# Two of three mLSTM chunk products on split rounded operands, with the heads' order rewritten

## The chip, the cores and the metric

The kernel runs on one core of a Trainium2 chip. The metric is the device time of one execution in microseconds (us), the median of several runs.

## What is computed

A trunk of two layers on x (1024 positions, width 1024). Layer 0 is an mLSTM mixer, layer 1 a pooling mixer; the change touches the chunk recurrence of layer 0 alone. Cut to that:

```python
proj = x @ w_in                                   # xm, z, o, gates
xc = silu(causal_dwconv(xm, conv_w, conv_b))
q = einsum(xch, w_q) * DK**-0.5;  k = einsum(xch, w_k);  v = einsum(xmh, w_v)
# 8 heads, DK 128, DV 256, 8 chunks of 128 positions; carry (C, n, m)
def step(carry, inp):
    ...
    s = einsum("bhtd,bhsd->bhts", qq, kk) * w_intra
    num = (einsum("bhts,bhsv->bhtv", s, vv)
           + w_inter[..., None] * einsum("bhtd,bhdv->bhtv", qq, C))
    den = s.sum(-1) + w_inter * einsum("bhtd,bhd->bht", qq, n)
    h = num / maximum(abs(den), exp(-m_t))[..., None]
    ...
    C_new = w_c[..., None, None] * C + einsum("bhs,bhsd,bhsv->bhdv", w_s, kk, vv)
```

## The kernel before

Everything large is a fp32 product made of rounded operands: each operand is split into a high part (rounded, type fp32r) and a low part (the rest, fp32r too), and `split()` in the TensorE block (L2774, L2775, L2776) issues three matmuls, high by high, high by low, low by high. The high part of a tile is written by ScalarE (`in_high`, L1153, and its like), the low part by VectorE as raw minus high (`in_low`, L1870).

Layer 0 walks through its input projection in 24 pairs of blocks, three pairs for a head (X_OF, Z_OF, O_OF), each pair in seven products (a Strassen scheme), 12 matmuls of 128x512 for a product. `PRODUCTS_A` is their order, `AT_A` its inverse; operands lie in a ring of four (`inb`). Between the products stands the rest of a head h:

- After product (O_OF, 5): `values(h)` makes v in 48 matmuls of 128x256, then `query_or_key` makes q and k in 24 of 128x512. Their operands are the parts of the head's qkv weights (`qkv`, high and low), of xm (`xm_hi`, and its low part in `xx_lo`) and of xc (`xc_hi`, and its low part in the other head's `xx_lo`).
- `CHUNK_AFTER` and `chunk_after` then put one chunk behind each of the next eight products. `chunk(h, c)` is `outputs(h, c)` and `scores(h, c + 1)`. `outputs` has three products in full fp32, 128x257 (v has 256 columns and one of ones): sT by v into `ps_intra` (L2946), qw by `state` added to it (L2949, not for chunk 0), and kw by v into `ps_state` (L2952, not for chunk 7). `scores` transposes a piece of k (L2931) and makes k by q for the next chunk (L2934), fp32 as well.
- Around it: `weighted_s` (VectorE, L1963) multiplies the scores by the decay weights `wgt` (ScalarE, `decay`, L1276) into sT; `weighted_k` (ScalarE, L1280) makes kw; `take_num` (ScalarE, L1284) copies the output; `next_state` (VectorE, L1991, L1993) updates `state`; `chunk_stats` (L1999), `scales` (L1969 to L1977), a power on GpSimd (`power`, L1031) and `norm_scale` (L1983, L1984) make the normalisation; the y_ and h_ steps make the branch output.

There is one sT, one kw, one wgt and one state, so each step waits for the reader of the one before. Every engine runs its instructions strictly in the order written down by hand: `first_half(h)`, `second_half(h)` and `next_head(h)` for ScalarE and for VectorE, where first_half(h) holds the chunks 1 to 7 of head h - 1; `first_layer_out` does the last head; long lists ahead of the loop do the start. SyncE issues the loads in one queue in the same way (`load_qkv`, `load_in`, `load_rows`, `store_h`). What reaches an engine early waits there behind whatever stands first.

## Time and profile before

| | before |
|---|---|
| median of 3 runs | 1404.59 us (1404.48 to 1404.92) |
| profiled execution, its own time | 1404.74 us |
| profiled execution, span of the trace | 1403.0 us |
| granted TensorE clock, mean | 0.998 of full speed |
| TensorE matmul busy | 1388.0 us, 99% |
| VectorE busy | 1119.1 us, 80% |
| ScalarE busy | 727.1 us, 52% |
| GpSimd busy | 152.4 us, 11% |

The span is what the trace covers of the one profiled execution, 1.7 us less than that execution's time. Layer 0 with its eight heads fills about the first 700 us of it; the recurrence stands between 89 and 699 us. A matmul's record is longer than its slot, since matmuls overlap: its cost is read from start to start. A fp32 matmul leaves two records.

### The profile page before, as it was taken

The numbers are of one execution on the slowest core, as the hardware profiler recorded it, in microseconds if no ns is written. First come the engines' busy times: TensorE is split into PE (matmuls) and PEld (weight loads), VectorE is DVE, ScalarE is ACT, GpSimd is POOL, SyncE is SP. The second block draws the span as 40 slices with busy tenths as digits, with TensorE's granted clock in tenths as the row PEclk, the third lists the DMA queues.
The fourth block names the chain that finished last, engine by engine and source line by source line (L and its number), as shares of the span: only waits on it lengthen the run. The fifth ranks groups of instructions, "written<-read, shape, count | busy, mean of one in ns | idle before, by whom it ended". The sixth has DMA issues, their size and how long they took to land.

```text
span 1403.0 us, 18567 instructions
## 1 busy us (share of the span) xinstructions
PE 1388.0 (99%) x6488; PEld 1155.2 (82%) x6488; DVE 1119.1 (80%) x1739; ACT 727.1 (52%) x1202; POOL 152.4 (11%) x251
## 2 busy tenths in 40 slices
PE   9999999999999999999999999999999999999997
PEld 7788888888888888888878888878888888888886
DVE  7988879798887978878674455797888888889976
ACT  6865646556564655656543345664333343336341
POOL 2002011110100111010000001001111111100021
PEclk9999999999999999999999999999999999999999
DMA  5024425353342534336487666444665555689661
GB/s 229 33 69 124 110 69 150 91 140 93 106 128 54 165 82 137 105 99 195 136 292 254 211 207 217 131 128 105 166 162 153 140 161 153 170 271 358 217 198 75
DMA packets 103435, 213.26 MB, mean 152 GB/s; under 512 B 10912, under 2 KB 27552, under 8 KB 102192
## 3 DMA queue, kind: packets, MB, share of 16 engines
q1 hardware_dynamic: 90544, 178.53, 38.4%
q0 software_dynamic: 12800, 33.56, 12.2%
q8 instruction: 52, 0.85, 0.2%
q14 instruction: 39, 0.32, 0.1%
HBM read 170.04 MB, written 75.56 MB: 175 GB/s over the span
## 4 chain that ended last, share of the span: by engine, by line
PE 62%; DVE 2%; DMA 1%; issue 0%; POOL 0%; ACT 0%; SPq 0%; DVEq 0%; POOLq 0%; ACTq 0%
PE wide L2774 13%; PE wide L2775 12%; PE wide L2776 12%; PE ps_state L2774 2%; PE ps_state L2775 2%; PE ps_state L2776 2%; PE ps_inter L2774 2%; PE ps_inter L2775 2%; PE ps_inter L2776 2%; PE ps_s L2774 1%; PE ps_intra L2774 1%; PE ps_s L2775 1%; PE ps_intra L2775 1%; PE ps_s L2776 1%; PE ps_intra L2776 1%; PE ps_intra L2946 1%
## 5 line engine op out<-in xcount | busy, mean ns | idle before, releaser
L2775 PE MATMUL wide<-xa,inb 128*128 128x512 f32 x576 | 224.5, 390 | 0.0
L2774 PE MATMUL wide<-xb,inb 128*128 128x512 f32 x472 | 189.3, 401 | 0.1
L2776 PE MATMUL wide<-xb,inb 128*128 128x512 f32 x472 | 184.3, 391 | 0.0
L2775 PEld LDWEIGHTS wide<-xa,inb 128*128 128x128 f32 x576 | 108.4, 188 | 19.7
L2775 PE MATMUL wide<-xa,blk 128*128 128x512 f32 x320 | 124.5, 389 | 0.0
L2776 PEld LDWEIGHTS wide<-xb,inb 128*128 128x128 f32 x472 | 88.6, 188 | 18.9
L2774 PEld LDWEIGHTS wide<-xb,inb 128*128 128x128 f32 x472 | 88.8, 188 | 18.0 <-DVE inb L1870 1.2
L2774 PE MATMUL wide<-xb,blk 128*128 128x512 f32 x256 | 99.7, 389 | 0.8 <-ACT zz L1741 0.8
L2776 PE MATMUL wide<-xb,blk 128*128 128x512 f32 x256 | 99.6, 389 | 0.0
L1789 ACT ACTIVATE wy<-wy_raw 128x1024 fp32r<-128x1024 f32 x56 | 59.4, 1062 | 61.9 <-DMA wy_raw<-y_block 61.6
L2774 PE MATMUL wide<-xa,inb 128*128 128x512 f32 x208 | 83.1, 400 | 2.8 <-DVE inb L1870 1.8
L2776 PE MATMUL wide<-xa,inb 128*128 128x512 f32 x208 | 81.2, 390 | 0.0
L2424 DVE TENSOR_TENSOR mw<-mw_raw,mw 128x1024 fp32r<-128x1024 f32 x53 | 63.0, 1220 | 20.0 <-ACT mw L1634 20.0
L2775 PEld LDWEIGHTS wide<-xa,blk 128*128 128x128 f32 x320 | 60.1, 188 | 12.5
L2677 DVE TENSOR_TENSOR wy<-wy_raw,wy 128x1024 fp32r<-128x1024 f32 x56 | 66.0, 1219 | 3.4 <-ACT wy L1789 3.1
L1646 ACT ACTIVATE blk<-a_raw 128x512 fp32r<-128x512 f32 x64 | 40.0, 627 | 44.3 <-PE wide L2776 21.6
L1923 DVE SCALAR_TENSOR_TENSOR xx<-xx,cols 128x1024 f32<-128x1024 f32 x48 | 61.4, 1280 | 1.5 <-ACT xx L1216 0.9
L1284 ACT ACTIVATE num<-ps_intra 128x257 f32<-128x257 f32 x64 | 24.6, 384 | 65.4 <-PE ps_state L2952 61.1
L1634 ACT ACTIVATE mw<-mw_raw 128x1024 fp32r<-128x1024 f32 x53 | 53.6, 1051 | 9.0 <-DMA mw_raw<-h_block 9.0
L2774 PEld LDWEIGHTS wide<-xb,blk 128*128 128x128 f32 x256 | 48.1, 188 | 11.2 <-issue 1.2
L2776 PEld LDWEIGHTS wide<-xb,blk 128*128 128x128 f32 x256 | 48.1, 188 | 9.9
L1629 ACT ACTIVATE stage<-wide 128x512 f32<-128x512 f32 x24 | 14.3, 597 | 79.1 <-PE wide L2776 78.5
(431 smaller groups left out, 3802.6 us busy)
## 6 DMA issues: line engine op xcount, KB each, us to landing
in_raw<-in_w_in SPq DMA_DIRECT2D x45, 512.0 KB, 4.3
wy_raw<-y_block SPq DMA_DIRECT2D x56, 256.0 KB, 4.4
mw_raw<-h_block SPq DMA_DIRECT2D x53, 256.0 KB, 3.4
m_sum<-in_w_out POOLq DMA_DIRECT2D x48, 256.0 KB, 4.6
h_block<-f_buf SPq DMA_DIRECT2D x48, 256.0 KB, 3.2
w_sum<-in_pool_w_out POOLq DMA_DIRECT2D x48, 256.0 KB, 4.3
a_raw<-in_pool_w_z SPq DMA_DIRECT2D x16, 512.0 KB, 4.0
a_raw<-folded SPq DMA_DIRECT2D x16, 512.0 KB, 4.4
```

Of the source, the lines that this page charges most:

```text
L1284: act.activation(num[:, c, :], ps_intra[:, 0:DV + 1], ACT.Copy).then_inc(num_taken, 1)
L1629: act.activation(dst[:, s % STAGES, :], spare_banks[spare_bank(("F", s))], ACT.Copy).then_inc(fold_taken, 1)
L1634: act.activation(hi, raw, ACT.Copy).then_inc(mw_hi, 1)
L1646: act.activation(blk_hi_at(i), block_raw(i), ACT.Copy).then_inc(blk_hi, 1)
L1789: act.activation(hi, raw, ACT.Copy).then_inc(wy_hi, 1)
L1923: ins = dve.scalar_tensor_tensor(out=xc_at(h, j), in0=xm_at(h, j, i), scalar=cols[:, at:at + 1], in1=xc_at(h, j), op0=ALU.mult, op1=ALU.add)
L2424: dve.tensor_tensor(lo, raw, hi.bitcast(F32), ALU.subtract).then_inc(mw_lo, 1)
L2677: dve.tensor_tensor(lo, raw, hi.bitcast(F32), ALU.subtract).then_inc(wy_lo, 1)
L2774: pe.matmul(dst, a[0], b[0], start=first, stop=False, skip_group_check=more)
L2775: pe.matmul(dst, a[0], b[1], start=False, stop=False, skip_group_check=more)
L2776: return pe.matmul(dst, a[1], b[0], start=False, stop=last, skip_group_check=more)
L2946: mm = pe.matmul(ps_intra[:, 0:DV + 1], sT[:, :], v, start=True, stop=c == 0)
```

## The change

`outputs` makes two of its three products on split rounded operands, each as three matmuls, hi by hi, hi by lo, lo by hi. The product with `state` stays fp32, as do the scores and the transpose.

```diff
-                mm = pe.matmul(ps_intra[:, 0:DV + 1], sT[:, :], v, start=True, stop=c == 0)
+                pe.matmul(ps_intra[:, 0:DV + 2], sT_hi[:, :], hi, start=True, stop=False)
+                pe.matmul(ps_intra[:, 0:DV], sT_hi[:, :], lo, start=False, stop=False)
+                mm = pe.matmul(ps_intra[:, 0:DV + 2], sT_lo[:, :], hi, start=False, stop=c == 0)
                 if c:
                     pe.wait_ge(state_ready, (NC - 1) * h + c)
                     mm = pe.matmul(ps_intra[:, 0:DV + 1], qw[:, tile(c)], state[:, :], start=False, stop=True)
                 if c < NC - 1:
-                    pe.wait_ge(kw_made, (NC - 1) * h + c + 1)
-                    mm = pe.matmul(ps_state[:, 0:DV + 1], kw[:, :], v, start=True, stop=True)
+                    pe.wait_ge(k_low, (NC - 1) * h + c + 1)
+                    pe.matmul(ps_state[:, 0:DV + 2], kw_hi[:, :], hi, start=True, stop=False)
+                    pe.matmul(ps_state[:, 0:DV], kw_hi[:, :], lo, start=False, stop=False)
+                    mm = pe.matmul(ps_state[:, 0:DV + 2], kw_lo[:, :], hi, start=False, stop=True)
```

The parts come from new steps. On ScalarE `weighted_k` writes kw and kw_hi, `round_s` writes sT_hi, and `round_v` rounds the upper half of v. On VectorE `low_s`, `low_k` and `low_v` write the low parts:

```diff
             def weighted_k(h, c):
                 act.wait_ge(s_full, NC * h + c + 1)
-                act.activation(kw[:, :], ps_inter[:, 0:P], ACT.Identity, scale=gcol_at(c, 3, h)).then_inc(kw_made, 1)
+                act.activation(kw[:, :], ps_inter[:, 0:P], ACT.Identity, scale=gcol_at(c, 3, h))
+                act.activation(kw_hi[:, :], ps_inter[:, 0:P], ACT.Identity, scale=gcol_at(c, 3, h)).then_inc(kw_made, 1)
+
+            def round_s(h, c):
+                act.wait_ge(s_taken, NC * h + c + 1)
+                act.activation(sT_hi[:, :], sT[:, :], ACT.Copy).then_inc(s_high, 1)
...
+            def low_s(h, c):
+                dve.wait_ge(s_high, NC * h + c + 1)
+                dve.tensor_tensor(sT_lo[:, :], sT[:, :], sT_hi[:, :].bitcast(F32), ALU.subtract).then_inc(chunk_low, 1)
+
+            def low_k(h, c):
+                dve.wait_ge(kw_made, (NC - 1) * h + c + 1)
+                dve.tensor_tensor(kw_lo[:, :], kw[:, :], kw_hi[:, :].bitcast(F32), ALU.subtract).then_inc(k_low, 1)
```

v's high parts lie in `xx_lo`; its low parts lie in `qkv`, in the place of the head's weights: for chunks 0 to 3 where the v weights were, taken straight from PSUM (`low_v(h, 0)` and `(h, 1)`, 128x512 each, ahead of the k products), for chunks 4 to 7 where the q and k weights were (`round_v(h, 0)` after k, `low_v(h, 2)`, 128x1024, then `round_v(h, 1)`). So the next head's weights are loaded later, and stand behind two `load_in` in SyncE's queue:

```diff
             def load_qkv(h):
                 if h:
-                    sp.wait_ge(k_full, 2 * h)
+                    sp.wait_ge(num_full, h * NC)
                 sp.dma_start(qkv_raw[:, 1, :], p_qkv[h, :, :]).then_inc(qkv_in, 16)
...
             for h in range(1, HEADS):
-                load_qkv(h)
                 load_in(3 * h + 1, 0)
                 load_in(3 * h + 1, 1)
+                load_qkv(h)
```

The lists of ScalarE and VectorE are written anew for the start, for each head and for the last head. Semaphores of layer 1 are shared with new ones of layer 0 by offsets; this moves no instruction.

TensorE in chunk 1 of the first head, before:

```order
L2946 MATMUL ps_intra<-xx,sT 128x257
L2949 MATMUL ps_intra<-state,qw 128x257
L2952 MATMUL ps_state<-xx,kw 128x257
L2931 MATMUL ps_inter<-ident,kT 128x128
L2934 MATMUL ps_s<-qT,kT 128x128
```

And now, in the next chunk of the same kind (the lines are those of the changed kernel):

```order
L3073 MATMUL ps_intra<-xx_lo,sT_hi 128x258
L3074 MATMUL ps_intra<-qkv,sT_hi 128x256
L3075 MATMUL ps_intra<-xx_lo,sT_lo 128x258
L3078 MATMUL ps_intra<-state,qw 128x257
L3081 MATMUL ps_state<-xx_lo,kw_hi 128x258
L3082 MATMUL ps_state<-qkv,kw_hi 128x256
L3083 MATMUL ps_state<-xx_lo,kw_lo 128x258
L3055 MATMUL ps_inter<-ident,kT 128x128
L3058 MATMUL ps_s<-qT,kT 128x128
```

Two fp32 matmuls have become six rounded ones; one fp32 matmul stands between them.

VectorE in the fourth head, from the weighting of chunk 5's scores (first row) to that of chunk 6's (second row with sT<-ps_s), before; in_low is the rows inb<-in_raw, norm_scale the two rows with small:

```order
L1963 TENSOR_TENSOR sT<-ps_s,wgt 128x128
L1870 TENSOR_TENSOR inb<-in_raw,inb 128x512
L1999 BN_STATS stats<-num 128x6
L1870 TENSOR_TENSOR inb<-in_raw,inb 128x512
L1983 TENSOR_TENSOR small<-small,rstd 128x4
L1984 SCALAR_TENSOR_TENSOR small<-mv,small 128x4
L2007 SCALAR_TENSOR_TENSOR o_buf<-o_buf,z_buf 128x512
L2013 TENSOR_TENSOR f_buf<-f_buf,z_buf 128x512
L1963 TENSOR_TENSOR sT<-ps_s,wgt 128x128
```

And now, from the last rows of `scales` (L2056 to L2058) to the low part of chunk 6's sT, on which TensorE waits:

```order
L2056 TENSOR_TENSOR small<-small 128x4
L2057 TENSOR_TENSOR small<-small,mv 128x4
L2058 TENSOR_SCALAR small<-small 128x4
L2080 BN_STATS stats<-num 128x6
L2064 TENSOR_TENSOR small<-small,rstd 128x4
L2065 SCALAR_TENSOR_TENSOR small<-mv,small 128x4
L2094 TENSOR_TENSOR f_buf<-f_buf,z_buf 128x512
L2024 TENSOR_TENSOR sT<-ps_s,wgt 128x128
L2088 SCALAR_TENSOR_TENSOR o_buf<-o_buf,z_buf 128x512
L2094 TENSOR_TENSOR f_buf<-f_buf,z_buf 128x512
L2044 TENSOR_TENSOR kw_lo<-kw,kw_hi 128x128
L2040 TENSOR_TENSOR sT_lo<-sT,sT_hi 128x128
```

`scales` has moved behind the weighting of chunk 5's scores, so norm_scale now follows it with one instruction between, and two steps of 128x512 stand between the weighting and the low part.

## Rows read from the trace of the kernel before

**Rows 1.** The page: the span, and each engine's busy time and instructions.

```profile
span 1403.0 us, 18567 instructions
PE 1388.0 (99%) x6488; PEld 1155.2 (82%) x6488; DVE 1119.1 (80%) x1739; ACT 727.1 (52%) x1202; POOL 152.4 (11%) x251
```

**Rows 2.** Busy time by stretch, fourth head: chunks, saturated stretch, all; clock, DMA.

```profile
336.73:367.25 30.52, 30.52 (x150) 25.72 (x148) 23.47 (x57) 15.94 (x38) 2.92 (x4) 1.00 0.24 61
...
376.15:410.57 34.42, 34.42 (x180) 29.41 (x179) 33.96 (x43) 22.88 (x34) 4.74 (x6) 1.00 0.55 151
...
336.73:419.31 82.58, 82.58 (x408) 69.68 (x407) 69.61 (x127) 48.54 (x90) 9.99 (x14) 1.00 0.39 109
```

**Rows 3.** Timeline of PE, first head, chunk 1 and product: start, length, instruction.

```profile
92.40 0.40 PE L2776 MATMUL wide<-xb,inb 128*128 128x512 f32 x1
92.63 0.60 PE L2946 MATMUL ps_intra<-xx,sT 128*128 128x257 f32 x2
93.07 0.59 PE L2949 MATMUL ps_intra<-state,qw 128*128 128x257 f32 x2
...
93.93 0.27 PE L2931 MATMUL ps_inter<-ident,kT 128*128 128x128 f32 x1
...
94.50 0.39 PE L2775 MATMUL wide<-xa,inb 128*128 128x512 f32 x1
...
97.00 0.60 PE L2946 MATMUL ps_intra<-xx,sT 128*128 128x257 f32 x2
```

**Rows 4.** Groups by line and shape, PE: records (two for each) and mean length.

```profile
L2946 PE MATMUL ps_intra<-xx,sT 128*128 128x257 f32 x128 | 38.3, 380 | 0.0
```

**Rows 5.** Timeline of PE: first matmul of values, and first after its 48.

```profile
74.33 0.28 PE L2774 MATMUL ps_state<-qkv,xm_hi 128*128 128x256 f32 x1
...
80.04 0.39 PE L2774 MATMUL wide<-xc_hi,qkv 128*128 128x512 f32 x1
```

**Rows 6.** Timeline of DVE, fourth head, chunks 4 and 5; scales, state, scores, stats.

```profile
352.94 0.15 DVE L1969 SCALAR_TENSOR_TENSOR small<-num,gcol 128x4 f32<-128x4 f32 x1
...
354.22 0.17 DVE L1977 TENSOR_SCALAR small<-small 128x4 f32<-128x4 f32 x1
355.31 0.48 DVE L1993 SCALAR_TENSOR_TENSOR state<-state,wc_bc,ps_state 128x257 f32<-128x257 f32 x1 [0.91 <-PE ps_state L2952]
355.70 0.28 DVE L1963 TENSOR_TENSOR sT<-ps_s,wgt 128x128 f32<-128x128 f32 x1
355.90 0.68 DVE L1870 TENSOR_TENSOR inb<-in_raw,inb 128x512 fp32r<-128x512 f32 x1
356.80 0.43 DVE L1999 BATCH_NORM_STATS2 stats<-num 128x6 f32<-128x256 f32 x1 [0.22 <-ACT num L1284]
357.15 0.67 DVE L1870 TENSOR_TENSOR inb<-in_raw,inb 128x512 fp32r<-128x512 f32 x1
357.74 0.15 DVE L1983 TENSOR_TENSOR small<-small,rstd 128x4 f32<-128x4 f32 x1
...
358.01 0.69 DVE L2007 SCALAR_TENSOR_TENSOR o_buf<-o_buf,z_buf 128x512 f32<-128x512 f32 x1
```

**Rows 7.** Timeline of POOL: the power between scales and norm_scale.

```profile
354.48 1.03 POOL L1031 TENSOR_TENSOR rstd<-small,nhalf 128x4 f32<-128x4 f32 x1 [8.48 <-DVE small L1977]
```

**Rows 8.** Timeline of ACT: weighted_k and the decay behind it.

```profile
360.47 0.36 ACT L1280 ACTIVATE kw<-ps_inter,gcol 128x128 f32<-128x128 f32 x1
360.72 0.40 ACT L1276 ACTIVATE wgt<-m_bc,gcol 128x128 f32<-128x128 f32 x1
```

**Rows 9.** Timeline of DVE, fourth head: low part of xm, first half.

```profile
403.04 1.22 DVE L1943 TENSOR_TENSOR xx_lo<-xx,xm_hi 128x1024 fp32r<-128x1024 f32 x1
```

**Rows 10.** Timeline of PE: values start, fourth head; a late product, fifth head.

```profile
404.93 0.28 PE L2774 MATMUL ps_state<-qkv,xm_hi 128*128 128x256 f32 x1
...
484.52 0.39 PE L2776 MATMUL wide<-xb,inb 128*128 128x512 f32 x1
485.04 0.50 PE L2774 MATMUL wide<-xb,inb 128*128 128x512 f32 x1
```

More of the change, by code:

```diff
@@ L341, in build @@
             bias = sA("bias", [P, 1])
+            sA("line_b", [P, 15])
+            sT_hi, kw_hi = (sA(name, [P, P], F32R) for name in ("sT_hi", "kw_hi"))
         with ExitStack() as own:
@@ L2097, in first_half @@
                 x = AT_A[3 * h + 2, 1] - 14
-                in_sum(3 * h, 3)
+                weighted_s(h - 1, 2)
                 in_join(3 * h - 1, 4)
                 next_state(h - 1, 1)
-                weighted_s(h - 1, 2)
+                chunk_stats(h - 1, 1)
+                in_sum(3 * h, 3)
+                low_s(h - 1, 2)
+                low_k(h - 1, 2)
+                y_factor_o(h - 1, 0)
+                y_factor_f(h - 1, 0)
                 gate_out_z(h - 1, 2)
                 gate_out_z(h - 1, 3)
-                y_factor_o(h - 1, 0)
@@ L2121, in first_half @@
-                in_low(x + 7)
                 chunk_stats(h - 1, 4)
-                in_low(x + 8)
                 norm_scale(h - 1, 0)
+                y_factor_f(h - 1, 1)
+                weighted_s(h - 1, 6)
                 y_factor_o(h - 1, 2)
                 y_factor_f(h - 1, 2)
-                weighted_s(h - 1, 6)
+                low_k(h - 1, 6)
+                low_s(h - 1, 6)
                 next_state(h - 1, 5)
-                chunk_stats(h - 1, 5)
                 y_factor_o(h - 1, 3)
-                in_sum(3 * h + 1, 0)
@@ L2222, in first_layer_out @@
                 in_low(AT_A[PAIRS_A - 1, 3])
+                group_lo(0)
+                weighted_s(last, 0)
+                low_s(last, 0)
                 weighted_q(last)
-                weighted_s(last, 0)
-                group_lo(0)
-                unit_lo(0)
+                low_k(last, 0)
+                low_v(last, 2)
+                gate_out_z(last, 2)
+                gate_out_z(last, 3)
+                chunk_stats(last, 0)
+                weighted_s(last, 1)
+                low_s(last, 1)
@@ L2227, in first_layer_out @@
+                next_state(last, 0)
+                low_k(last, 1)
+                unit_lo(0)
+                unit_lo(1)
+                in_join(PAIRS_A - 1, 4)
+                next_state(last, 1)
+                low_k(last, 2)
+                weighted_s(last, 2)
+                low_s(last, 2)
+                weighted_s(last, 3)
+                low_k(last, 3)
                 y_factor_o(last, 0)
                 y_factor_f(last, 0)
-                next_state(last, 0)
-                weighted_s(last, 1)
@@ L2242, in first_layer_out @@
+                unit_lo(3)
+                weighted_s(last, 4)
                 y_factor_o(last, 1)
+                next_state(last, 3)
+                low_s(last, 4)
+                low_k(last, 4)
                 y_factor_f(last, 1)
                 y_factor_o(last, 2)
-                next_state(last, 3)
-                weighted_s(last, 4)
-                chunk_stats(last, 1)
-                chunk_stats(last, 2)
+                next_state(last, 4)
+                weighted_s(last, 5)
@@ L2249, in first_layer_out @@
+                low_s(last, 5)
+                unit_lo(4)
+                low_k(last, 5)
                 chunk_stats(last, 3)
-                unit_lo(3)
-                weighted_s(last, 5)
                 scales(last, 0)
-                next_state(last, 4)
-                y_factor_f(last, 2)
-                unit_lo(4)
+                norm_scale(last, 0)
                 weighted_s(last, 6)
-                norm_scale(last, 0)
                 next_state(last, 5)
                 unit_lo(5)
+                low_k(last, 6)
@@ L2260, in first_layer_out @@
+                low_s(last, 6)
                 chunk_stats(last, 4)
+                y_factor_f(last, 2)
                 y_factor_o(last, 3)
@@ L2358, in _ @@
             in_low(15)
+            in_join(2, 2)
+            low_xc(0, 1)
+            low_xc(0, 0)
+            low_v(0, 0)
+            low_v(0, 1)
             in_join(2, 5)
-            gate_out_z(0, 1)
+            in_low(16)
+            weighted_s(0, 0)
+            gate_out_z(0, 0)
             weighted_q(0)
-            weighted_s(0, 0)
+            low_k(0, 0)
+            low_s(0, 0)
             in_sum(3, 0)
             in_sum(3, 1)
-            in_low(16)
             in_sum(3, 2)
@@ L2368, in _ @@
             next_state(0, 0)
+            gate_out_z(0, 1)
+            low_s(0, 1)
             chunk_stats(0, 0)
             in_low(17)
+            low_k(0, 1)
+            low_v(0, 2)
             for h in range(1, HEADS):
```

484 lines of the change are left out of this document (276 added, 208 removed).

## The prediction

> **What bounds the kernel now.** I read the page's busy shares first: TensorE is busy for 1388.0 of 1403.0 us, so the span is TensorE's own work and a cut of it is worth its full size unless something new makes TensorE wait [rows 1]. Then the busy time by stretch, for one head: over 82.58 us TensorE has no gap, while VectorE is busy for 69.61 and ScalarE for 48.54. But VectorE's idle time lies unevenly: in the 30.5 us of the chunks it is busy for 23.5, in the 34.4 us ahead of values for 34.0, which is no room at all [rows 2]. Last the timelines, from start to start, since records overlap and a short wait of TensorE doesn't show as a gap: one product in the fifth head starts 0.52 us after the matmul before it, where 0.23 is the slot, so about 0.3 us was lost there while VectorE ran late [rows 10]. VectorE's order is therefore the second thing to watch, TensorE's work the first.
>
> **Step 1, TensorE's matmuls.** What goes: from 92.63 to 93.93 us stand three fp32 products of 257 columns, 1.30 us, so 0.433 us each [rows 3]. What comes: values issues 48 rounded matmuls of 256 columns in 80.04 - 74.33 = 5.71 us, 0.119 us each [rows 5]; the 512 column ones run at (97.00 - 94.50) / 11 = 0.227 us [rows 3], so two columns more cost about 0.001 us, and the three matmuls of a split product 0.120 + 0.119 + 0.120 = 0.359 us. A product gains 0.074 us. There are 128 / 2 = 64 products with sT [rows 4], and by the code seven of eight chunks have one with kw, 56: 120 in all, 120 x 0.074 = **8.9 us** less on TensorE, all of it on the path.
>
> The bounds of the rate: 258 columns are shown by no row. Below lies the 256 column slot, 0.119 us; above, the 512 column one, 0.227 us, with which 240 matmuls of 258 columns would cost 26 us more. I take 0.120, since the row differs from it in two columns and nothing else.
>
> The Trainium skill, page "TensorE: Matmul & The Clock Gate", section "Back-to-back issue gap", gives a spacing of the column count divided by 2.4 GHz plus about 2.5 ns. By that a matmul of 256 or 258 columns would take about 0.110 us, a split product 0.330, and the gain would be 12 us. This trace doesn't agree: 0.119 for 256 columns and 0.227 for 512 [rows 3, 5].
>
> **Step 2, switches between the two kinds.** Into fp32 the slot is 92.63 - 92.40 = 0.23 us, so nothing is seen. Out of it: from 93.93 to 94.50 stand three records of 128 columns and one rounded matmul. A 257 column record takes 0.217, so a 128 column one about 0.108; 3 x 0.108 + 0.227 = 0.55, which leaves 0.02 for a switch there and back [rows 3]. Chunks 1 to 6 gain two switches each (the fp32 product with state now stands between rounded ones): 48 pairs x 0.02 = 1.0 us at most, 0 at least. I take **0.9 us** back, so 8.0 us remain.
>
> **Step 3, the new work of the other engines.** VectorE's price is 0.20 us for 128x128 (355.70 to 355.90) and 0.59 for 128x512 (357.15 to 357.74) [rows 6], so about 1.13 for 128x1024 (its 1.22 us record [rows 9] less the same 0.09 of overlap). A head adds 8 low_s, 7 low_k, two low_v of 512 and one of 1024: 15 x 0.20 + 2 x 0.59 + 1.13 = 5.3 us. ScalarE adds 7 second kw, 8 round_s at 0.25 to 0.36 [rows 8] and two of 1024 columns at about 1.0 each, some 6 us. Idle are 82.6 - 69.6 = 13 and 34 us of a head [rows 2], so both fit by amount. By place: low_s, low_k and low_v(h, 2) fall in the chunks, where VectorE has 7.0 us idle for 4.1 us of new work; low_v(h, 0) and (h, 1) fall between the end of values and the k products, while q is made (12 x 0.23 = 2.8 us), which covers them and the two copies out of PSUM ahead of them. The load of the next weights waits for the last chunk now and is used by ScalarE some 15 us later; behind it wait one load_in and the rows of decays, with time to spare. I cost all of these at nothing; without cover it would be the 5.3 us a head.
>
> **Step 4, the chain ahead of a chunk.** TensorE used to need one VectorE step after the scores; now it needs three in a row, weighted_s, round_s, low_s: 0.28 + 0.36 + 0.28 plus two handovers, about 1.05 us. The cover is one product, 12 x 0.227 = 2.73 us [rows 3], less some 0.17 us until the scores are in PSUM (a record outlasts its slot by 0.16). What stands between them on VectorE's list decides. Adding up the list for chunks 1 to 5 and 7, the low part comes 0.05 to 0.8 us ahead of TensorE; chunk 2 is the closest (the scores' weighting, a join, the state, the statistics, a sum: 0.20 + 0.60 + 0.39 + 0.35 + 0.60, then the low part). Chunk 6 comes out late. Put t = 0 where TensorE starts chunk 5; a chunk took 94.50 - 0.23 - 92.63 = 1.64 us [rows 3] and takes 1.64 - 0.15 + 0.02 = 1.51 now, so chunk 6 wants to start at 1.51 + 2.73 = 4.24. The scores of chunk 5 came at -2.55 (chunk 4 started 4.24 earlier, its block and 0.18 us of landing make 1.69). ScalarE writes kw twice and then sT_hi, 0.25 + 0.25 + 0.36, so low_s(5) runs at -1.65 to -1.45; state 0.39 and low_k 0.20 bring -0.85; scales takes 354.22 + 0.17 - 352.94 = 1.45, to 0.60 [rows 6]; the power starts 0.09 later and takes 1.03, to 1.72 [rows 7]. Only chunk_stats (0.35) lies beside it, so VectorE stands idle for some 0.8 us, and norm_scale starts at 1.8. Then 0.27 for it, 0.60 for y_factor_f, weighted_s at 2.67, two steps of 0.60 and low_k: low_s(6) starts at 4.27 and ends at 4.55. TensorE waits about **0.3 to 0.4 us**. In the kernel before, 3.3 us of other work lay between scales and norm_scale, and TensorE needed only the weighting. Seven heads have this list (the last one has its own, with fewer steps there): 7 x 0.4 = **2.8 us**. Bounds: 0 if each step is a little shorter than I count, 5 us if chunk 2 joins in with 0.3 us.
>
> **Step 5, the saturated stretch.** In the fourth head the low part of xm ended at 403.04 + 1.22 = 404.26, values began at 404.93 [rows 9, 10]. Behind the weighting of chunk 7, the new list has 0.6 + 0.2 + 0.35 + 0.6 us more to do (in_low, low_s, chunk_stats, in_sum) and 0.4 less (a state), 1.3 us net; of the 5.5 us that a head's VectorE idles outside the two stretches of rows 2, about a half lies there and most of it can be used, and in_low(x + 20) stands 1.1 us earlier against its neighbours. I find low_xm about 0.8 us ahead of TensorE, so no new wait; the waits of before in two heads, some 0.6 us, may go or stay. I count 0.3 us of gain, from 0 to 0.6.
>
> **The sum.** Profiled execution 1404.74 = span 1403.0 + 1.7. Less 8.9, plus 0.9, plus 2.8, less 0.3: 5.5 us less, 1399.2; the median of the runs lies 0.15 below the profiled one: **1399.0 us**, from 1396.3 (no new wait) to 1401.7 (5 us of waits, rounded matmuls as priced).
>
> **The rivals.**
> - *All is hidden.* The chain for chunk 6 fits after all and no wait comes. For it: VectorE idles 13 us a head [rows 2]. Against it: the power's 1.03 us [rows 7] has almost nothing beside it. 1404.6 - 8.3 = 1396.3 us.
> - *The gain is eaten.* The chain is late for most chunks by a little: 8.0 / 56 = 0.14 us for each chunk of 56 is enough to eat all, and my margins at chunks 1 and 2 are 0.2 and 0.05. For it: one sT, one wgt and a strict order, so that a late step of ScalarE holds VectorE too. 1404 us, within 1401.8 to 1407.4.
> - *Slower: the saturated stretch overflows.* Where the chunks' new 4.1 us aren't taken up in idle time, VectorE enters the stretch ahead of values late, and there is nothing to catch up with: 34.0 of 34.4 us are busy [rows 2]. It decides from about 0.8 us of lateness on; with 2.6 us late (half of a head's new work), 1.8 us x 7 heads = 12.6 us go. On top of the forecast, 1399.0 + 12.6 = 1412 us. The late product in the fifth head speaks for it [rows 10].
> - *The rate isn't what values shows*: 258 columns priced as 512, 1399.0 + 26 = 1425 us. Nothing but the missing row speaks for it.
>
> **How the numbers follow.** Forecast 0.58, all hidden 0.16, eaten 0.14, overflow 0.10, rate 0.02. The range goes from 1395.9 to 1404.5: it takes in the forecast, the hidden case and most of the eaten one. Some 0.2% (2.8 us) is what a measurement of this kernel tells from no change: faster means under 1401.8, slower over 1407.4. The first two cases give 0.74 less a little of the forecast's upper edge, 0.73; eaten and that edge 0.15; the last two 0.12.
>
> **What would show it.** Right: matmuls of 258 columns 0.120 us apart; blocks of chunks 1 to 6 of 1.51 us instead of 1.64; one late start a head, at chunk 6, of 0.3 to 0.4 us, released by VectorE's sT_lo; VectorE idle on GpSimd's rstd by some 0.8 us a head; no new wait at values. Wrong: the late starts elsewhere or none, a pitch of heads over 82.3 us, a rounded matmul of over 0.13 us, or a wait for the loads behind load_qkv.

## The result and the profile after

The change made the kernel slower: 1414.72 us (1412.36 to 1415.05) against 1404.53 us (1404.1 to 1404.92) of the kernel before in the same comparison, a ratio of 1.0069 with a 95% interval of 1.0052 to 1.0086. One of the ten executions of experiment 6 took 4477.9 us and is left out of its ratio; nothing else below was disturbed like that. The forecast was 1399.0, the range ended at 1404.5; the sign was wrong.

The page after, to be laid beside [rows 1]:

```profile
span 1412.6 us, 19112 instructions
PE 1387.5 (98%) x6608; PEld 1153.4 (82%) x6608; DVE 1159.2 (82%) x1883; ACT 771.8 (55%) x1338; POOL 152.4 (11%) x251
```

TensorE is busy for about as long as before, which says little here: a record of TensorE outlasts its slot, and hides short gaps. VectorE has 40 us more and is at 82% instead of 80. The place of the loss is read from TensorE's waits (line waited for, releaser: us in total, times, longest):

```profile
PE ps_inter L3094 <- ACT num L1328: 6.6, 7, 1.5
PE ps_intra L3073 <- DVE sT_lo L2040: 1.6, 4, 0.5
PE wide L2898 <- DVE z_buf L1968: 1.4, 4, 0.5
```

The first row is new and the largest. It is the turn of the normalised head's second half (`turn_head`'s third, behind the product that follows chunk 7), which waits for ScalarE's `norm_head(h-1, 1)`. "The taps" below are VectorE's steps of the convolution, `xx<-xx,cols` in the trace; the product behind them needs a join (`z_buf<-wide,z_buf`) that stands after them in VectorE's list. "Values" is the stretch of 48 matmuls that makes v, and a head's pitch is the time from its chunk 0 to the next head's.

**By head.** Adding up starts of TensorE that come more than 0.1 us late, over the seven heads from chunk 0 to chunk 0: the third turn 7.65 us (0.82 to 0.91, in two heads 1.64 and 1.66), chunk 0 2.24 (four heads), the product behind the taps 2.03 (four heads), chunk 6 1.98 (0.26 to 0.30 in each). In the kernel before it was 0.6 in all. The sum of the seven pitches went from 578.8 to 587.7 us, 8.9 of the span's 9.6. Of what is outside them, chunk 0 of the first head starts 0.46 us later (89.16 instead of 88.70), and the last head's turn waits 1.25 instead of 0.44. Windows of the fourth head, its chunks and from chunk 7 to values (length, then busy time of PE, PEld, DVE, ACT, POOL), first before, then after:

```profile
336.73:367.25 30.52, 30.52 (x150) 25.72 (x148) 23.47 (x57) 15.94 (x38) 2.92 (x4) 1.00 0.24 61
367.25:404.93 37.68, 37.68 (x173) 31.22 (x172) 35.30 (x57) 22.27 (x34) 6.33 (x7) 1.00 0.56 154
```

```profile
340.49:370.63 30.14, 30.00 (x162) 25.64 (x163) 25.60 (x69) 19.84 (x52) 2.93 (x4) 1.00 0.19 46
370.63:410.56 39.93, 38.05 (x174) 31.04 (x173) 36.64 (x60) 20.52 (x30) 6.20 (x7) 1.00 0.62 170
```

The chunks became shorter by 0.4 us, with a wait of 0.3 us at chunk 6 in them; experiment 5, which takes this wait away, makes it 0.8. The stretch behind chunk 7 became 2.25 longer, and VectorE, called full there, is idle for 3.3 us of it (2.4 before). It isn't short of time, it waits itself.

**What was right.** TensorE in chunk 1 of the first head (beside [rows 3]): matmuls of 258 and 256 columns start 0.12 us apart, and the state's fp32 product among them costs nothing to be seen (measured as the prediction did it, chunk 5 of the fourth head takes 358.84 - 0.23 - 357.12 = 1.49 us, against 1.64 before and 1.51 forecast):

```profile
93.03 0.28 PE L3073 MATMUL ps_intra<-xx_lo,sT_hi 128*128 128x258 f32 x1
93.15 0.28 PE L3074 MATMUL ps_intra<-qkv,sT_hi 128*128 128x256 f32 x1
93.27 0.28 PE L3075 MATMUL ps_intra<-xx_lo,sT_lo 128*128 128x258 f32 x1
93.39 0.59 PE L3078 MATMUL ps_intra<-state,qw 128*128 128x257 f32 x2
```

Chunk 6 of the fourth head, VectorE first, then TensorE, which should have started at 365.60:

```profile
363.07 0.16 DVE L2064 TENSOR_TENSOR small<-small,rstd 128x4 f32<-128x4 f32 x1 [0.83 <-POOL rstd L1054]
...
365.56 0.29 DVE L2040 TENSOR_TENSOR sT_lo<-sT,sT_hi 128x128 fp32r<-128x128 f32 x1
```

```profile
365.37 0.39 PE L2900 MATMUL wide<-xb,inb 128*128 128x512 f32 x1
365.90 0.39 PE L3073 MATMUL ps_intra<-xx_lo,sT_hi 128*128 128x258 f32 x1
366.12 0.28 PE L3074 MATMUL ps_intra<-qkv,sT_hi 128*128 128x256 f32 x1
```

0.30 us late, VectorE idle for 0.83 on GpSimd's power: step 4, to the place and the size. The first matmul after such a wait also takes 0.22 us to the next instead of 0.12. Its weight load starts at 365.89, together with it; that of the matmul at 365.37 started 0.22 us ahead of it.

**What was missed.** The same head behind chunk 7 (370.63). Before, where chunk 7 started at 367.25, VectorE's `scales` began at 372.71, and ScalarE's norm_head ran at 376.27:

```profile
372.11 0.68 DVE L1893 TENSOR_TENSOR inb_raw<-in_raw 128x512 f32<-128x512 f32 x1
372.71 0.16 DVE L1969 SCALAR_TENSOR_TENSOR small<-num,gcol 128x4 f32<-128x4 f32 x1
```

```profile
376.27 2.08 ACT L1289 ACTIVATE num<-num,small 128x256 f32<-128x256 f32 x4 [1.24 <-DVE small L1984]
```

```profile
379.47 0.60 PE L2963 MATMUL ps_inter<-ident,num 128*128 128x128 f32 x4
```

So it ended at 378.35 and TensorE came at 379.47: 1.1 us to spare. After, on VectorE, GpSimd, ScalarE and TensorE:

```profile
374.14 0.69 DVE L1954 TENSOR_TENSOR sum_t<-in_raw 128x512 f32<-128x512 f32 x1 [0.70 <-DMA in_raw<-in_w_in]
...
376.98 0.69 DVE L1931 TENSOR_TENSOR inb<-inb_raw,inb 128x512 fp32r<-128x512 f32 x1
377.58 0.74 DVE L2104 SCALAR_TENSOR_TENSOR o_buf<-ps_s,cols,o_buf 128x512 f32<-128x512 f32 x1
378.24 0.68 DVE L1968 TENSOR_TENSOR xx<-wide,xx 128x512 f32<-128x512 f32 x1
378.84 0.16 DVE L2050 SCALAR_TENSOR_TENSOR small<-num,gcol 128x4 f32<-128x4 f32 x1
```

```profile
380.39 1.40 POOL L1054 TENSOR_TENSOR rstd<-small,nhalf 128x4 f32<-128x4 f32 x1 [11.61 <-DVE small L2058]
```

```profile
382.22 2.08 ACT L1328 ACTIVATE num<-num,small 128x256 f32<-128x256 f32 x4 [1.49 <-DVE small L2065]
```

```profile
382.57 0.39 PE L2900 MATMUL wide<-xb,inb 128*128 128x512 f32 x1
384.44 0.63 PE L3094 MATMUL ps_inter<-ident,num 128*128 128x128 f32 x4 [1.48 <-ACT num L1328]
```

`scales` starts 8.21 us behind chunk 7 instead of 5.46. 0.70 of the 2.75 is a wait for a load: it is issued only 1.5 us ahead of chunk 7, since it waits for in_low(x+8), which now stands behind chunk 7's weighting, and it took 5.0 us in this head and in the seventh, 3.5 to 4.2 in the others. 1.26 are in_low(x+11) and y_turned(h-1, 1), which now stand ahead of scales; the rest comes of the other y_ steps that do, y_turned(h-1, 0) and y_finish(h-1, 0). In heads without the wait for the load norm_head starts 10.8 us behind chunk 7 instead of 9.0, and the 1.1 us to spare become 0.8 of wait.

**The waits behind the taps** have a second cause beside the longer list. Once a head GpSimd lays a mask over `m_bc`, and VectorE's steps beside it take longer. In the first, third, fourth and fifth heads the mask makes one of them longer by 0.61 to 0.83 us, and these are the four heads where the product behind the taps is late; in the second, sixth and seventh it costs 0.24 or 0.25, and the product is in time. The fifth and the sixth head have VectorE's steps in the same order and to within 0.06 us at the same distance from chunk 7 up to this place. The mask in each, then VectorE beside it:

```profile
468.19 1.10 POOL L1083 TENSOR_SCALAR_AFFINE_SELECT m_bc<-m_bc 128x1024 f32<-128x1024 f32 x1 [1.80 <-DMA qw<-wi_rows]
...
553.14 1.14 POOL L1083 TENSOR_SCALAR_AFFINE_SELECT m_bc<-m_bc 128x1024 f32<-128x1024 f32 x1 [3.58 <-DMA qw<-wi_rows]
```

```profile
468.39 1.44 DVE L1931 TENSOR_TENSOR inb<-in_raw,inb 128x512 fp32r<-128x512 f32 x1 [0.86 <-ACT inb L1176]
...
552.63 0.69 DVE L1931 TENSOR_TENSOR inb<-in_raw,inb 128x512 fp32r<-128x512 f32 x1 [0.86 <-ACT inb L1176]
553.23 0.75 DVE L2104 SCALAR_TENSOR_TENSOR o_buf<-ps_inter,cols,o_buf 128x512 f32<-128x512 f32 x1
553.90 0.92 DVE L1931 TENSOR_TENSOR inb<-in_raw,inb 128x512 fp32r<-128x512 f32 x1
```

Two steps on the fifth head is 0.55 us behind the sixth, and its product behind the taps is 0.5 us late. In the kernel before the mask cost VectorE 0.9 us in four heads and no product behind the taps was late: the shift of the list used up the spare time, and the mask's place then decided.

### The profile page after: what moved, and what is told of

The parts are those of the page before. It is cut to its first block, busy times and chain, and to the rows that moved or that the text cites. A ratio compares the mean times of both kernels' runs of the same rounds, so it can differ in the third digit from the quotient of the medians.

```text
span 1412.6 us, 19112 instructions
## 1 busy us (share of the span) xinstructions
PE 1387.5 (98%) x6608; PEld 1153.4 (82%) x6608; DVE 1159.2 (82%) x1883; ACT 771.8 (55%) x1338; POOL 152.4 (11%) x251
## 4 chain that ended last, share of the span: by engine, by line
PE 73%; issue 12%; DVE 6%; DMA 3%; ACT 2%; POOL 2%; SPq 0%; DVEq 0%; POOLq 0%; ACTq 0%
PE wide L2898 15%; PE wide L2900 15%; PE wide L2899 15%; PE ps_state L2898 3%; PE ps_state L2900 3%; PE ps_state L2899 3%; PE ps_inter L2899 2%; PE ps_inter L2898 2%; PE ps_inter L2900 2%; DMA in_raw<-in_w_in 2%; PE ps_intra L2900 2%; PE ps_s L2898 2%; PE ps_intra L2898 2%; PE ps_s L2900 2%; PE ps_s L2899 2%
## 5 line engine op out<-in xcount | busy, mean ns | idle before, releaser
L1931 DVE TENSOR_TENSOR inb<-in_raw,inb 128x512 fp32r<-128x512 f32 x70 | 49.9, 725 | 8.7 <-ACT inb L1176 8.6
```

The lines of the kernel that those rows point to most:

```text
L1931: dve.tensor_tensor(inb[:, i % RING_A, 1, :], in_source(i), inb[:, i % RING_A, 0, :].bitcast(F32), ALU.subtract).then_inc(in_lo, 1)
```

## The experiments

Times are medians; each ratio is to the kernel before, run beside it. Where waits and pitches are given, they are those of the one profiled execution. Run 3 is that of experiment 3, and so on. Lines left out inside a code cut are marked with dots. A wait "at the turn" is the third turn's.

**1. The rounding by itself.** In the kernel before, the first seven heads get the three rounded matmuls on constant tiles of the input, so that nothing has to make the parts; what these heads compute is left out by it.

```diff
-                mm = pe.matmul(ps_intra[:, 0:DV + 1], sT[:, :], v, start=True, stop=c == 0)
...
+                def three(b, last):
+                    pe.matmul(b[:, 0:DV + 2], known[0], known[1], start=True, stop=False)
+                    pe.matmul(b[:, 0:DV], known[0], known[1][:, 0:DV], start=False, stop=False)
+                    return pe.matmul(b[:, 0:DV + 2], known[0], known[1], start=False, stop=last)
+
+                if h < HEADS - 1:
+                    mm = three(ps_intra, c == 0)
...
```

> The kernel before, where in heads 1 to 7 the two products of outputs are three rounded matmuls each on constant tiles of the input (258, 256 and 258 columns), with the old lists and the old waits; nothing makes the split parts, so the branch of these heads is not computed. It measures steps 1 and 2 alone. Theory (the matmuls gain what was forecast, the loss is elsewhere): 105 of the 120 products, 7/8 of 8.0 us less, 7.0 us, about 1397.6 us, block of chunks 1 to 6 1.51 us instead of 1.64. Rival (258 columns or the switches cost more in this place): 1402 us or over.

1398.23 us, ratio 0.9956 (0.9942 to 0.9970), as expected. Steps 1 and 2 hold: the rounding is worth 6.3 us in seven heads, where they give 7.0. The loss is in the rest.

**2. The reverse.** The changed kernel with fp32 products of the high parts.

```diff
-                pe.matmul(ps_intra[:, 0:DV + 2], sT_hi[:, :], hi, start=True, stop=False)
-                pe.matmul(ps_intra[:, 0:DV], sT_hi[:, :], lo, start=False, stop=False)
-                mm = pe.matmul(ps_intra[:, 0:DV + 2], sT_lo[:, :], hi, start=False, stop=c == 0)
+                whole = hi.bitcast(F32)[:, 0:DV + 1]
+                mm = pe.matmul(ps_intra[:, 0:DV + 1], sT_hi[:, :].bitcast(F32), whole, start=True, stop=c == 0)
...
```

> The changed kernel with its lists, its splits and all its waits, but each split product done as one fp32 matmul of the high parts (257 columns); the low parts are made and not used. TensorE's work is that of the kernel before again. Theory (at the turn TensorE waits for a chain of VectorE and DMA steps that doesn't hang on its own speed in the chunks): of the 8 us that the matmuls cost more, most disappear in the waits, 1414 to 1418 us. Rival (each part adds by itself): 1414.7 + 8 = 1422.7 us.

1418.95 us, 1.0098 (1.0083 to 1.0114): one us above what the waits' theory gave, well under the 1422.7 of plain adding. From chunk 7 to values the seven heads take 273.9 us, the same as with rounded products; the chunks take 216.8 instead of 210.9. So the new orders and steps cost about 14 us over the kernel before, and the rounding gives back 4 here, since some of it runs into waits.

**3. The norm's scales earlier.** `scales(h-1, 1)` directly behind `chunk_stats(h-1, 7)`, `norm_scale(h-1, 1)` behind `in_sum(3h+1, 1)`, on ScalarE `norm_head(h-1, 1)` ahead of `in_high(x+12)`.

```diff
                 chunk_stats(h - 1, 7)
+                scales(h - 1, 1)
                 y_finish(h - 1, 0)
                 in_sum(3 * h + 1, 0)
                 in_sum(3 * h + 1, 1)
+                norm_scale(h - 1, 1)
...
-                scales(h - 1, 1)
                 y_finish(h - 1, 1)
-                norm_scale(h - 1, 1)
...
```

> The changed kernel with the second scales and norm_scale of a head moved ahead of the four in_sum (scales directly behind chunk_stats of chunk 7) and norm_head(h - 1, 1) moved ahead of in_high(x + 12) on ScalarE. Theory A (the loss is TensorE waiting 0.8 to 1.7 us a head at the third turn for norm_head, because scales, the power and norm_scale come late in VectorE's list): the 8.6 us of these waits go, nearly nothing comes back: 1404.5 to 1407 us. Theory B (VectorE is simply full, the overflow rival: lateness moves on to the products ahead of values): the waits move there, under 3 us gained, 1411.5 us or over.

1411.37 us, 1.0043 (1.0028 to 1.0058). No wait at the turn is left in the seven heads, but the product behind the taps now comes 5.3 us late in all instead of 2.0. Between the theories, and close to the second: the turn's wait was real, and nearly half of what it gave was lost some 10 us further on.

**4. The load earlier.** `in_low(x+8)`, whose operand the next load overwrites, behind `next_state(h-1, 5)`.

> The changed kernel with in_low(x + 8) moved from behind weighted_s(7) to behind next_state(5), so that SyncE's load of the next block, which waits for it, is issued some 1.5 to 2 us earlier. Theory A' (the late load holds the first in_sum, and with it scales): VectorE's wait of 0.7 us for the load goes, the third turn's wait falls by about 0.7 us a head, 7 x 0.7 = 4.9 us, 1410 us. Rival (the load only just covers other lateness, the list itself is too long there): under 1.5 us gained, 1413 us or over.

1410.37 us, 1.0042 (1.0027 to 1.0057), the time that was expected. The turn's waits fell from 7.65 to 4.51 us, less than the expected 4.9, and those behind the taps rose from 2.0 to 3.5 in this execution, in which the mask costs VectorE 0.78 to 0.88 us in six heads; in these the product is late, in the other it is not.

**5. Chunk 6's list.** `norm_scale(h-1, 0)` behind `weighted_s(h-1, 6)`, and `y_factor_f(h-1, 2)`, one of the two steps of 128x512 ahead of low_k and low_s, behind `next_state(h-1, 5)`.

```diff
                 chunk_stats(h - 1, 4)
-                norm_scale(h - 1, 0)
                 y_factor_f(h - 1, 1)
                 weighted_s(h - 1, 6)
+                norm_scale(h - 1, 0)
                 y_factor_o(h - 1, 2)
-                y_factor_f(h - 1, 2)
                 low_k(h - 1, 6)
                 low_s(h - 1, 6)
                 next_state(h - 1, 5)
+                y_factor_f(h - 1, 2)
...
```

> The changed kernel with norm_scale(0) moved behind weighted_s(6), and y_factor_f(2) behind next_state(5), so that low_s(6) comes about 1 us earlier. The wait of 0.3 us at chunk 6 goes in seven heads. Theory A says that this gives little or nothing by itself, since TensorE then comes to the third turn earlier and waits there for the same VectorE chain, which is held by the load and the list: 1413.5 to 1415 us. Rival (each wait is lost by itself and adds): 7 x 0.3 = 2.1 us, 1412.5 us.

1409.7 us, 1.0037 (1.0023 to 1.0052). The waits at chunk 6 are gone and the chunks take 208.1 us instead of 210.9. That is 2.8, and 5.0 came off the time; the turn's waits fell too (7.65 to 5.87). A gain at one place isn't eaten here; both theories had expected less.

**6. The three together.**

> The changed kernel with the three moves of a1, a2 and a3 together. After the single moves, theory H (head of line: TensorE's waits come from a few VectorE steps that stand in the list behind a DMA landing, a power or the taps, not from a lack of VectorE time): the third turn's and chunk 6's waits go together, those at chunk 0 (2.2 us in all) and at the product behind the taps (2 to 4 us) stay: 1402 to 1405 us. Theory B (VectorE is full): its lateness collects at the product behind the taps, 1407 us or over.

1405.46 us, 1.0004 (0.9995 to 1.0014): the kernel before is reached, at the upper edge of what the theory of places gave (1402 to 1405). Pitches of 82.1 to 82.9 us; what is left lies at chunk 0 (1.6 in all) and behind the taps (4.0).

**7 and 8. Two further moves, alone and on top.** `in_sum(3h+3, 0)` behind chunk 0's low parts, and `in_join(3h+1, 5)` ahead of the last tap.

```diff
-                in_sum(3 * h + 3, 0)
                 low_s(h, 0)
                 low_k(h, 0)
+                in_sum(3 * h + 3, 0)
```

> The changed kernel with the last two moves of a5 alone: in_sum(3h + 3, 0) behind low_s(0) and low_k(0), and in_join(3h + 1, 5) ahead of the third tap. Theory H: the waits at chunk 0 (2.2 us) and behind the taps (2.0 us) go, and nothing is given back at the turn beyond 1 us, since their stretches lie far apart: 1410.5 to 1412 us. Rival (one VectorE chain through the whole head): 1413.5 us or over.

> The five moves: those of a4, in_join(3h + 1, 5) ahead of the third tap, and in_sum(3h + 3, 0), which waits for a load, behind low_s(0) and low_k(0). VectorE and ScalarE do the same work as in the changed kernel. Theory H: no wait of size is left in the heads, pitch 81.6 to 82.0 us, and the time comes to what m1 measured for the matmuls alone, 1396.5 to 1400 us, faster than the kernel before. Theory B: VectorE's 5 us more a head have to show, pitch 82.5 us or over, 1404 us or over.

1416.57 us (1.0084, 1.0070 to 1.0097) alone, 1406.87 us (1.0020, 1.0011 to 1.0029) on top: 1.9 and 1.4 us more than without them, and both numbers as the rivals had them. The waits at chunk 0 went, but the join now stood in VectorE's list before what it waits for was done and held the list up (VectorE is idle ahead of it for about 1 to 1.5 us), and TensorE waited at values in every head:

```profile
PE ps_state L2898 <- DVE xx_lo L2004: 3.3, 7, 0.5
```

So the first of the two moves does what it should at its place, and the second is bad.

**9. SyncE's order.** `load_in(3h+2, 0)` ahead of `load_qkv(h)`.

```diff
-                load_qkv(h)
                 load_in(3 * h + 2, 0)
+                load_qkv(h)
```

> The changed kernel with two lines of SyncE's list exchanged in each head: load_in(3h+2, 0) is issued ahead of load_qkv(h), which waits until the last chunk's scales for the rows are read. Theory (a queue held by its head): the late load holds in_low(x+14) on VectorE, 1.58 us idle in one head of the last trace, and through it the join and the product behind the taps, where TensorE waits 0.35 to 0.63 us in four heads; these go, the third turn's waits of 0.8 us a head stay. Time 1412.5 to 1414.0 us, 0.5 to 2 us under the changed kernel. Rival (the late product comes from VectorE's own list, and the load has no part in it): no change, 1414.7 within 0.5.

1414.68 us, 1.0068 (1.0056 to 1.0081): no change, as the rival had it. The load isn't issued sooner (5.7 us behind chunk 7 in most heads, as without the exchange), since it waits for VectorE's four sums anyway. The product behind the taps is late in six heads here, and again in those six where the mask makes a VectorE step longer by 0.6 us or more; in the fourth head it costs 0.27, and the product is in time.

**10. Five moves:** 3, 4, 5, the first of 7, and 9.

> The changed kernel with five moves in the orders and no operation taken out or added: scales and norm_scale of the second half directly behind their sums and ScalarE's norm_head(1) ahead of in_high; norm_scale(h-1, 0) behind weighted_s(6); in_low(x+8) behind next_state(5); in_sum(3h+3, 0) behind low_s(h, 0) and low_k(h, 0); load_in(3h+2, 0) ahead of load_qkv(h). Theory A (single places of the order are late, VectorE's sum of work is not the bound): the three moves tried together left a pitch of 82.7 us a head, with waits at chunk 0 (0.1 to 0.5) and behind the taps (0.2 to 1.0); the two further moves take most of them, pitch 81.7 to 82.1 us, time 1398 to 1402 us, faster than the kernel before. Theory B (the stretch ahead of values is full, so what is saved at one place comes back at another): the waits only change place, time 1404 to 1407 us as with three moves.

1404.93 us (1402.60 to 1409.20), 1.0005 (0.9996 to 1.0014): taken alone, this is what the theory of a full VectorE gave (1404 to 1407), and not the 1398 to 1402 of the theory of places. Chunk 0 is in time in every head; behind the taps 4.5 us are left, in one head 0.14 and in another 1.53.

**11. Seven moves:** also `in_join(3h+1, 5)` behind the last tap and, in the last head, norm_head ahead of a load's rounding.

> The last kernel with two more moves: in_join(3h+1, 5) on VectorE directly behind the last tap, ahead of y_turned(h-1, 3), and in the last head norm_head(last, 1) ahead of mw_high(5) on ScalarE. Theory A: the product behind the taps finds its rows in time and the last turn's wait of 1.24 us falls by 0.4 to 0.8: 0.5 to 2 us under the run with five moves, 1397 to 1401 us. Theory B (y_turned's tile is then late for TensorE or for the values instead): no gain, or up to 2 us above the run with five moves.

1402.71 us, 0.9984 (0.9975 to 0.9992), 2.2 under the run with five, and short of the expected 1401; the last turn's wait didn't fall. Three heads have a pitch of 81.6 us, 1.0 less than before; the others have 82.4 to 83.8. What sets them apart is when `load_in(3h+2, 0)` lands. It is issued 6.9 us behind chunk 7 in each; in the order of the heads it takes 6.3, 4.4, 4.3, 6.9, 5.3, 4.4 and 5.6 us, and TensorE is late behind the taps by 1.16, 0, 0, 1.78, 0.36, 0 and 0.63. In the fourth head, the load's issue, its landing, ScalarE and TensorE:

```profile
371.85 0.33 SPq L753 DMA_DIRECT2D in_raw<-in_w_in  x1
```

```profile
DMA to landing us min/median/max: 6.9/6.9/6.9
```

```profile
378.76 1.15 ACT L1176 ACTIVATE inb<-in_raw 128x512 fp32r<-128x512 f32 x2 [3.28 <-DMA in_raw<-in_w_in]
```

```profile
388.00 0.47 PE L2898 MATMUL wide<-xb,inb 128*128 128x512 f32 x1 [1.63 <-DVE z_buf L1968]
```

In the kernel before it was issued 5.6 us behind chunk 7: move 3 puts 1.4 us of scales ahead of the sums that it waits for.

**12. The load without its neighbours**: the weights of qkv and the rows of decays, 1.5 MB that were issued right behind it, are loaded behind `load_in(3h+2, 1)`. **13. And sooner**: `y_finish(h-1, 0)` behind the sums.

```diff
                 load_in(3 * h + 2, 0)
-                load_qkv(h)
-                load_rows(h)
                 store_h(h - 1, 1, 2)
                 load_in(3 * h + 2, 1)
+                load_qkv(h)
+                load_rows(h)
```

> The kernel with seven moves, and on SyncE the load of the qkv weights and the two rows of decays (3 x 512 KB, so far directly behind load_in(3h+2, 0)) put behind load_in(3h+2, 1). Theory (the late product behind the taps hangs on the landing of that one load): in the run with seven moves it is issued 6.89 us after chunk 7 and takes 4.3 to 6.9 us; the heads where it took 4.3, 4.4 and 4.4 lost nothing, those with 5.3, 5.6, 6.3 and 6.9 lost 0.36, 0.63, 1.16 and 1.78. Without the other three loads beside it, it takes 3.6 to 4.8 us in every head, all seven pitches come to 81.6 to 81.9 us, and the time to 1397.5 to 1400 us. Rival (how long that load takes has nothing to do with the loads beside it, or VectorE's own lateness makes the wait): 3.9 to 7 us for the load as before, pitches spread from 81.6 to 83.8, 1402 to 1403.5 us.

> The last kernel, and y_finish(h-1, 0) on VectorE taken from ahead of the four in_sum(3h+1) to behind in_join(3h, 4), so that load_in(3h+2, 0), which waits for these sums, is issued 0.6 us sooner (6.3 us after chunk 7). Theory (the landing of the load): what still is late in the run before falls by 0.6 us a head, no head late, 1397 to 1399.5 us; if nothing was late any more, no change within 0.5 us. Rival (VectorE's list): no change, 1402 to 1403.5.

1404.76 us (1.0004, 0.9995 to 1.0013) and 1404.17 us (0.9996, 0.9987 to 1.0005): both missed the times of their theories, and 12 is 2 us slower than 11. In 12 the load still took 4.0 to 5.6 us; that it is slow by its neighbours isn't shown. Behind the taps nothing over 0.11 us was left in either, and in each head 0.6 us had appeared at values. So the landing alone hadn't made the waits of 11: the load of the seventh head took 5.6 us in both, with 0.63 us of wait in 11 and none in 12. What 12 had taken away from the stretch between this load and the taps is the mask, which had cost VectorE 0.7 to 0.9 us there. In 13, GpSimd and VectorE of the fourth head:

```profile
389.16 1.59 POOL L1083 TENSOR_SCALAR_AFFINE_SELECT m_bc<-m_bc 128x1024 f32<-128x1024 f32 x1 [16.51 <-DMA qw<-wi_rows]
```

```profile
389.12 0.69 DVE L1954 TENSOR_TENSOR sum_t<-in_raw 128x512 f32<-128x512 f32 x1
389.72 1.58 DVE L1931 TENSOR_TENSOR inb<-sum_v,inb 128x512 fp32r<-128x512 f32 x1
391.22 0.68 DVE L1954 TENSOR_TENSOR inb_raw<-sum_t,in_raw 128x512 f32<-128x512 f32 x1
```

GpSimd masks the rows once a head, as soon as they have landed, and the VectorE step beside it takes 1.58 us instead of 0.69. Loading the rows later had moved this 0.9 us from 15.5 to 17.9 us behind chunk 7, where VectorE soon waits for others, to some 23 us, where nothing is left to take it up.

**14. The rows between**: 13 with `load_rows(h)` back ahead of `load_in(3h+2, 1)`, behind the stores.

```diff
                 store_h(h - 1, 1, 2)
+                load_rows(h)
                 load_in(3 * h + 2, 1)
                 load_qkv(h)
-                load_rows(h)
```

> The last kernel (a12) with the two rows of decays loaded ahead of load_in(3h+2, 1), behind store_h(h-1, 1, 2), instead of behind it; the load of the qkv weights stays behind it. In a12 the lateness behind the taps was gone, and a wait of 0.6 us at values came in every head. Theory (VectorE and GpSimd hold each other up): the mask that GpSimd lays over m_bc (1.1 us, once a head) starts when the rows have landed; in a12 that is 22.5 to 23.6 us after chunk 7, beside a VectorE tensor_tensor of 128x512 that takes 1.58 us instead of 0.68, in the stretch ahead of values, where VectorE has no room; in the run with seven moves it was 15.5 to 17.9 us after chunk 7, beside a gate's product (2.00 instead of 1.28 us), where VectorE had to wait for ScalarE a little later anyhow. With the rows loaded earlier the mask falls at 16 to 19 us, the values wait goes, all seven pitches come to 81.6 to 81.9 us and the time to 1397 to 1399.5 us. Rival (the wait at values comes from the later load of qkv or from y_finish, not from the mask): values wait of 0.6 us stays, pitch 82.5, 1403.5 to 1405 us.

1399.20 us (1397.55 to 1400.60), ratio 0.9959 (0.9946 to 0.9973), as expected and 5 us less than 13 by moving two loads. The waits at values, 4.4 us in the profile of 13, are gone. The pitches are 81.75, 81.61, 81.62, 81.61, 81.61, 81.62 and 81.84. The fourth head as a whole (columns as in the windows above, beside the last row of [rows 2]), the mask, and TensorE entering values without a step:

```profile
333.45:415.06 81.61, 81.61 (x424) 69.46 (x422) 74.88 (x146) 53.99 (x108) 10.01 (x14) 1.00 0.39 110
```

```profile
380.79 1.27 POOL L1083 TENSOR_SCALAR_AFFINE_SELECT m_bc<-m_bc 128x1024 f32<-128x1024 f32 x1 [11.66 <-DMA qw<-wi_rows]
```

```profile
400.45 0.39 PE L2900 MATMUL wide<-xb,inb 128*128 128x512 f32 x1
400.68 0.28 PE L2898 MATMUL ps_state<-qkv,xm_hi 128*128 128x256 f32 x1
```

VectorE does 74.88 us of work in a pitch of 81.61, and TensorE doesn't wait for it once. The changed kernel has the same steps (74.80 in its fourth head) and needed 84.45.

## Why the prediction was wrong

- **Steps 1 and 2, right.** 258 columns take 0.120 us and a split product 0.36, so the row had been the better guide than the spacing for isolated matmuls of the Trainium skill's page "TensorE: Matmul & The Clock Gate", section "Back-to-back issue gap" (0.330). The undisturbed heads of run 14 are 81.61 us against 82.68 on average before, 7.5 us for seven; the steps give 8.0 x 7/8 = 7.0 and 0.6 of waits of before that go, 7.6. The rate rival is out. The 0.9 us for switches of step 2 can't be seen.
- **Step 3, wrong in its last sentences.** The amounts were right: VectorE's page time grew by 40 us against 8 x 5.3 = 42. "With time to spare" was wrong for the loads, though not where I looked: load_qkv itself held nobody up (run 9). The load of in_raw that waits for in_low(x+8), moved behind the weighting of chunk 7, was 0.7 us late for the sums in two heads; I didn't follow it.
- **Step 4, right for chunk 6** (0.26 to 0.30 us a head, forecast 0.3 to 0.4) and for chunks 1 to 5 and 7, which are in time; the last head, left out of the count, was 0.2 us late at chunk 6 too. It ended at chunk 7. The chain for chunk 0, with `in_sum(3h+3, 0)` between the weighting and low_s, was not added up: 2.2 us.
- **Step 5 failed, and this decides.** It put the net work of VectorE behind chunk 7 (1.3 us) against TensorE's arrival at values, 35 us later, and found 0.8 us to spare. But TensorE takes something from this list at least three times on the way: the third turn 12 us behind chunk 7, with 1.1 us to spare in the profile of before, the product behind the taps, and values. The shift of 1.8 us, in two heads 2.6, hit the first of these: 7.65 us, the largest term of the loss. Behind the taps it met the mask on GpSimd, of which the prediction has no term: 2.0 us. "I count 0.3 us of gain" stands in place of 7.65 + 2.0 of loss.
- **The overflow rival** had named the stretch and nearly the time (1412), but not the cause: "nothing to catch up with". VectorE is idle for 3.3 us of the 39.93 from chunk 7 to values, and run 14 fits the same steps into 37.60. It wasn't a lack of VectorE's time but the places of some eight of its steps and of two loads.
- **The sum.** The profiled execution took 1414.5 us, 15.3 over the 1399.2. By place: third turn 7.65, chunk 0 2.24, behind the taps 2.03, the last turn 0.8, the gain of step 5 that didn't come 0.3, less 0.8 at chunk 6: 12.2. In the first head the mask fell beside the low part of xm (2.11 us instead of 1.22) and made a product ahead of the chunks 0.6 us late, which didn't happen in runs 12 and 14; the last head's chunk 6 gives 0.2. Behind each of the 15 late starts of a chunk or of the product behind the taps, the next matmul comes 0.1 us later too, as at 365.90 above, which makes 1.5; behind a turn it is 0.03, which makes 0.2. About 0.6 us has no place; the four executions of the changed kernel lie up to 2.7 us apart.

That run 14 lies at the time I had forecast (1399.2 to 1399.0) is partly chance: the forecast had 2.8 us of waits at chunk 6, which run 14 hasn't, and the last head's turn is 0.8 us later than forecast.

Open: run 12 doesn't tell why the load's time varies from 3.5 to 6.9 us. How the gain of run 14 over 11 divides between the load's landing and the mask isn't told apart in full either: between 13 and 14 the mask's place is worth 4.4 us at values in the profiles, of 5 in the medians, and a load of 5.6 us made TensorE wait only where the mask stood behind it. The last head's turn (1.2 us) was not brought forward; the one move tried there changed nothing.

## What to carry to other kernels

When a change lengthens an in-order list, write down every consumer of that list with its time to spare in the old profile, and hold the shift against each of them in the order of time, the nearest first; a check at the far end of the stretch misses those on the way. An engine that is 80% busy with strict lists is not full: the same steps cost 84.0 or 81.7 us a head by their order and that of the loads. A load or a helper engine's step that is "anywhen" has a place too, as it can slow down the list beside it.

## What the runs showed of the hardware

**VectorE and GpSimd stand in each other's way.** The mask (128x1024) takes 1.1 us alone; a VectorE step with two inputs in SBUF that falls beside it takes longer by up to 0.9: 128x512 1.58 us instead of 0.69 (run 13), 128x1024 2.00 instead of 1.28 (run 11). In the kernel before it was there too:

```profile
379.98 1.24 POOL L1060 TENSOR_SCALAR_AFFINE_SELECT m_bc<-m_bc 128x1024 f32<-128x1024 f32 x1 [3.14 <-DMA qw<-wi_rows]
```

```profile
379.57 0.69 DVE L2029 TENSOR_TENSOR f_buf<-o_buf,f_buf 128x512 f32<-128x512 f32 x1
380.18 1.58 DVE L1870 TENSOR_TENSOR inb<-sum_t,inb 128x512 fp32r<-128x512 f32 x1
```

The ends tell more than the lengths. Here the step ends 0.54 us after the mask, whose end is 381.22. In the profiles of before, after, and runs 11 to 14 there are 48 masks, and in 47 a VectorE step with two SBUF inputs ends behind the mask: by 0.54 or 0.55 us where it writes 128x512 and by 1.07 or 1.08 where it writes 128x1024, whenever its record started. So it does its work after the mask, not slower beside it. It goes the other way as well: a mask that starts while such a step is under way mostly ends 0.95 to 1.01 us after that step's end, and later still where another one gets in ahead of it. Its record is up to 2.3 us long between the heads, and 4.8 us in the first head of run 14, beside five such steps in a row. The power takes 1.40 us at 380.39 of the kernel after and at 374.26 of the kernel before, where VectorE's y_finish was under way, against 1.03 [rows 7]. The Trainium skill, page "SBUF — State Buffer", section "SBUF: two separate sides", says that the two share a pair of ports as an exclusive lock for the whole instruction, and that on VectorE's side an operation with two SBUF inputs takes it against a GpSimd operation that reads SBUF. The traces agree, by the ends above. They also show the other side: `o_buf<-ps_inter,cols,o_buf`, 128x512 with one of its two large inputs in PSUM, took 0.75 us at 553.23 of the kernel after, in the middle of the mask at 553.14, as it does elsewhere (0.73 to 0.75), and the mask wasn't held up by it.
